# Dilated score products on 64 rows of the array, items in pairs of heads

## What is computed

```
q_nope, q_rope = q[..., :64], rope(q[..., 64:96])          # "mla": 96 features a head
s = (q_nope @ k_nope + q_rope @ k_rope) * 96 ** -0.5       # causal, blocks of 128 queries
o_mla = softmax(s) @ v_mla                                 # 64 features a head
qd, kd, vd = 8 heads of 64 features; qd, kd = rope(qd), rope(kd)
o_dil = mix over windows (128, 1), (512, 4), (2048, 16) of softmax(qd @ kd) @ vd
```

## Time and profile before

| | |
|---|---|
| median of 3 runs | 3322.12 us (3318.78 to 3323.09) |
| the profiled execution | 3324.39 us, of which the span of the profile is 3322.6 us |
| mean granted TensorE clock | 0.959 of full |
| PE, PEld busy | 3011.2 us (91%), 2524.6 us (76%) |
| DVE, ACT, POOL busy | 1620.6 us (49%), 1219.5 us (37%), 296.5 us (9%) |
| DMA | mean 73 GB/s |

### The profile page before, as it was taken

How to read it: one execution, slowest core, us unless ns; L and a number is a source line. 1 busy time by engine, 2 the same in 40 slices (tenths; PEclk the granted TensorE clock), 3 DMA queues, 4 the chain that set the end, 5 groups by cost and what they waited for, 6 DMA issues and landing times. The chain is left out here.

```text
span 3322.6 us, 40007 instructions
## 1 busy us (share of the span) xinstructions
PE 3011.2 (91%) x15598; PEld 2524.6 (76%) x15598; DVE 1620.6 (49%) x2744; ACT 1219.5 (37%) x2044; POOL 296.5 (9%) x274
## 2 busy tenths in 40 slices
PE   5798879989799999978899999899999778999997
PEld 3676879868578888855688888788888646888886
DVE  5744455442544443536564434654435275644336
ACT  4423544322333322335543323533223345432224
POOL 0000057620000000011000000000000020000000
PEclk9899989999899999989999999999999899999998
DMA  7111000012223333210123232132332200233321
GB/s 240 57 58 44 1 12 1 1 32 95 63 76 104 101 96 101 89 51 1 49 78 97 95 102 95 58 108 95 96 107 83 70 1 33 72 100 98 99 95 58
DMA packets 66860, 241.95 MB, mean 73 GB/s; under 512 B 7408, under 2 KB 9584, under 8 KB 66032
## 3 DMA queue, kind: packets, MB, share of 16 engines
q1 hardware_dynamic: 66672, 239.38, 22.3%
HBM read 236.21 MB, written 3.15 MB: 72 GB/s over the span
## 5 line engine op out<-in xcount | busy, mean ns | idle before, releaser
L220 PE MATMUL pair<-h_hi_at,w_hi_at 128*128 128x512 f32 (+1 forms) x2048 | 782.1, 382 | 45.4 <-DVE h_lo_at L410 30.6
L222 PE MATMUL pair<-h_hi_at,w_lo_at 128*128 128x512 f32 (+1 forms) x2048 | 760.5, 371 | 0.0
L221 PE MATMUL pair<-h_lo_at,w_hi_at 128*128 128x512 f32 (+1 forms) x2048 | 760.4, 371 | 0.0
L188 DVE TENSOR_TENSOR w_lo_at<-w_raw,w_hi_at 128x1024 fp32r<-128x1024 f32 x350 | 436.8, 1251 | 472.2 <-ACT w_hi_at L180 472.1
L180 ACT ACTIVATE w_hi_at<-w_raw 128x1024 fp32r<-128x1024 f32 x350 | 366.0, 1052 | 537.1 <-PE pair L222 521.3
L220 PEld LDWEIGHTS pair<-h_hi_at,w_hi_at 128*128 128x128 f32 x2048 | 389.8, 190 | 121.7 <-DVE h_lo_at L410 37.0
L221 PEld LDWEIGHTS pair<-h_lo_at,w_hi_at 128*128 128x128 f32 x2048 | 390.3, 191 | 67.1
L222 PEld LDWEIGHTS pair<-h_hi_at,w_lo_at 128*128 128x128 f32 x2048 | 389.9, 190 | 65.4
L2144 DVE TENSOR_TENSOR work_at<-pair,rstd_at 128x512 f32<-128x512 f32 (+1 forms) x184 | 122.1, 667 | 363.4 <-PE pair L222 363.3
L220 PE MATMUL pair<-a_hi_at,w_hi_at 128*128 128x512 f32 (+1 forms) x792 | 290.1, 366 | 0.0
L221 PE MATMUL pair<-a_lo_at,w_hi_at 128*128 128x512 f32 (+1 forms) x792 | 289.4, 365 | 0.0
(11 more groups left out here) (395 smaller groups left out, 4423.2 us busy)
## 6 DMA issues: line engine op xcount, KB each, us to landing
w_raw<-in_weights SPq DMA_DIRECT2D x433, 512.0 KB, 3.5
residual<-in_x SPq DMA_DIRECT2D x1, 2048.0 KB, 10.4
cos_sin_at<-rope_table SPq DMA_DIRECT2D x2, 1024.0 KB, 5.1
out<-residual SPq DMA_DIRECT2D x16, 128.0 KB, 1.7
rope_table<-table SPq DMA_DIRECT2D x1, 1024.0 KB, 11.1
ctx_in<-in_ctx SPq DMA_DIRECT2D x1, 1024.0 KB, 5.0
mask_at<-in_layer_masks SPq DMA_DIRECT2D x2, 512.0 KB, 4.3
levels<-in_levels SPq DMA_DIRECT2D x1, 896.0 KB, 4.5
```

The lines of the kernel that those rows point to most:

```text
L188: eng.tensor_tensor(self.w_lo[:, g % self.split].rearrange("p k n -> p (k n)"), self.w_raw[:, g % RAW], self.w_hi[:, g % self.split].rearr ...
L220: pe.matmul(out, sh, mh, start=start, stop=False)
L221: pe.matmul(out, sh, ml, start=False, stop=False)
L222: return pe.matmul(out, sl, mh, start=False, stop=stop)
```

## The change

The padded copy goes away: `qd` is rotated in place, as one addition of 128 rows a tile, and the instruction that clears `q_wide` is left out. The score product of a dilated item takes 64 rows of `qd` and the same 64 rows of `kd`: rows 0 to 63 for an even head, 64 to 127 for an odd one. The items of both kinds come in pairs of heads: two heads of block 0, the same two of block 1, and so on, so that widths run 128, 128, 256, 256, 384, 384, 512, 512. PE's order becomes one by pairs: `score(i)`, `score(i + 1)`, `turn(i - 2)`, `turn(i - 1)`, `weigh(i - 4)`, `weigh(i - 3)`. The programs of DVE and ACT and all waits are unchanged.

```diff
-def rope(kit, items, clear, copy=None, room=None):
+def rope(kit, items, clear=None, copy=None, room=None):
...
-                act.activation(clear, kit.squares[:, 0, 0:1][:, :, None].to_broadcast(clear.shape), ACT.Copy,
-                               scale=0.0).then_inc(cleared, 1)
+                if clear is not None:
+                    act.activation(clear, kit.squares[:, 0, 0:1][:, :, None].to_broadcast(clear.shape), ACT.Copy,
+                                   scale=0.0).then_inc(cleared, 1)
...
-def attention(kit, items, sink, room=None):
+def attention(kit, items, sink, room=None, paired=False):
...
+                if paired:
+                    for i in range(0, n + 4, 2):
+                        for job, j in ((score, i), (turn, i - 2), (weigh, i - 4)):
+                            if 0 <= j < n:
+                                job(j)
+                                job(j + 1)
+                    return
                 lag = ahead - 1
                 for i in range(n + lag + 2):
...
-         + [(qd[:, t], [(rows, q_wide[rows, 2 * t + i]) for i, rows in enumerate(halves)], dil) for t in range(4)],
-         clear=q_wide[:, :, :], copy=(kh[HD:HD + 32, :, :],
+         + [(qd[:, t], qd[:, t], dil) for t in range(4)],
+         copy=(kh[HD:HD + 32, :, :],
...
-    kinds = ((qh[0:96], kh[0:96], 1, vm, o_lat, (HD + 32) ** -0.5), (q_wide, kd, 2, vd, o_dil, HD ** -0.5))
-    items = [dict(head=h, q=q[:, h, n * P:(n + 1) * P], pieces=[(k[:, h // per_tile, 0:(n + 1) * P], 0)],
...
-    attention(kit, items, sink=False, room=Room(kit, H_UNIT))
+    def item(kind, head, n, q, k, v, out, scale):
...
+    items = [item(0, h, n, qh[0:96, h], kh[0:96, h], vm, o_lat, (HD + 32) ** -0.5)
+             for t in range(4) for n in range(4) for h in (2 * t, 2 * t + 1)]
+    items += [item(1, 2 * t + i, n, qd[rows, t], kd[rows, t], vd, o_dil, HD ** -0.5)
+              for t in range(4) for n in range(4) for i, rows in enumerate(halves)]
+    attention(kit, items, sink=False, room=Room(kit, H_UNIT), paired=True)
```

More of the change, by code:

```diff
@@ L2713, in interior @@
     project_kv(kit, (lat_split[0][:, 2], lat_split[1][:, 2]), kh, vm)
-    q_wide = kit.delta
     halves = (slice(0, HD), slice(HD, P))
@@ L2719, in interior @@
          + [(kd[:, t], kd[:, t], dil) for t in range(4)]
-         + [(qd[:, t], [(rows, q_wide[rows, 2 * t + i]) for i, rows in enumerate(halves)], dil) for t in range(4)],
-         clear=q_wide[:, :, :], copy=(kh[HD:HD + 32, :, :],
+         + [(qd[:, t], qd[:, t], dil) for t in range(4)],
+         copy=(kh[HD:HD + 32, :, :],
                                       k_rope[HD:HD + 32, :][:, None, :].to_broadcast([32, 8, SEQ])), room=Room(kit, WORK_UNIT))
-    kinds = ((qh[0:96], kh[0:96], 1, vm, o_lat, (HD + 32) ** -0.5), (q_wide, kd, 2, vd, o_dil, HD ** -0.5))
-    items = [dict(head=h, q=q[:, h, n * P:(n + 1) * P], pieces=[(k[:, h // per_tile, 0:(n + 1) * P], 0)],
-                  width=(n + 1) * P, values=[v[:, b, h * HD:(h + 1) * HD] for b in range(n + 1)],
-                  mask=mask[:, kind, 512 - (n + 1) * P:512], out=out[:, n, h * HD:(h + 1) * HD], scale=scale)
-             for kind, (q, k, per_tile, v, out, scale) in enumerate(kinds) for h in range(8) for n in range(4)]
-    attention(kit, items, sink=False, room=Room(kit, H_UNIT))
+    def item(kind, head, n, q, k, v, out, scale):
+        w = (n + 1) * P
+        return dict(head=head, q=q[:, n * P:w], pieces=[(k[:, 0:w], 0)], width=w, scale=scale,
+                    values=[v[:, b, head * HD:(head + 1) * HD] for b in range(n + 1)], mask=mask[:, kind, 512 - w:512],
+                    out=out[:, n, head * HD:(head + 1) * HD])
+    items = [item(0, h, n, qh[0:96, h], kh[0:96, h], vm, o_lat, (HD + 32) ** -0.5)
[3 more added lines that the diff above has]
+    attention(kit, items, sink=False, room=Room(kit, H_UNIT), paired=True)
     at = layer * KD
```

## The result

The changed kernel takes 3475.43 us (median of 4 runs, 3470.45 to 3478.35), the kernel before 3322.61 us beside it. The ratio is 1.046, with a 95% interval of 1.0442 to 1.0478. It is 153 us slower where 54 were forecast: the direction was right, the size about a third of what came. The profiled execution has a span of 3471.8 us and a mean TensorE clock of 0.921 (before: 0.959).

What follows compares the result with a forecast made beforehand. PE was taken as the bound; the new order's round trip adds 29.9 us a layer, rope takes off 2.9, so 27.0 a layer, 54.0 in all: 3376.1 us, range 3355 to 3403.

Steps and rivals of the forecast that it cites:

- What bounds the kernel: Attention stage: PE's real work at full clock is the bound, busy 94.6 of 98.7 us.
- the pairing pays: Rival: attention stays bound by PE's work, rope's 2.9 and scores' 8.5 us come off per layer, 3299 us; chance 0.05.
- Rope: Rope stage, bound by DVE: single additions 1.89 us apart, last 0.69 us long; stage ends 2.9 us earlier.
- Score products: Dilated half: 64-row pairs save 8.5, 4.3 or 0 us of PE time a layer, hidden beside the round trip.
- the drain: Dilated half: changing PE's tiling mode drains the engine, 0 to 4.2 us a layer; taken as 0.
- Order of PE: Attention: each pair costs a full round trip, rounds 3.71, 4.40, 3.34, 4.45 us; stage 128.6 against 98.7 us.
- the named wait: Attention: turn(i - 1) waits for item i - 3's copy, behind exp(i) on ACT; over 1 us each.
- the loop: Attention: round trip from a pair's scores through DVE and ACT back to PE, 15.9 us per two heads against 11.8.
- The clock: Attention: PE's clock stays at 1.00, as in rope when busy 1.12 of 2 us; chance of a fall 0.08.
- The clock's price: Dilated half at clock 0.50: PE terms double, 7.5 us more per two heads, 60 us in all.
- The range: Total time: 3355 to 3403 us, widened from 3358 to 3400, leaving out a clock fall.
- the clock case: Rival: clock falls to 0.50 in the dilated half, 60 us more, total 3436 us; chance 0.08.

Runs made afterwards that it cites:

- e2: Changed kernel with PE's old order (score i, turn i-3, weigh i-5), 64-row products and paired items kept: 3331.93 us, ratio 1.0038.
- e3: Changed kernel with a deeper pair order: scores i, i+1, turns i-3, i-2, weighs i-5, i-4: 3319.37 us, ratio 0.9997.
- e8: Changed kernel with PE order score i, i+1, turn i-3, weigh i-5, turn i-2, weigh i-4: 3306.97 us, ratio 0.9956.
- e9: Changed kernel with padded queries and 128-row scores back, PE order score i, i+1, turn i-3, weigh i-5, turn i-2, weigh i-4: 3316.48 us.
- e6_same: Changed kernel with dilated pairs made of two heads on the same 64 rows, so their score products can't overlap: 3475.87 us, ratio 1.0462.
- e1_order: Changed kernel with padded queries and 128-row score products back, pair order kept: 3415.03 us, ratio 1.0283.
- e5_act: Changed kernel with ACT's copy of item i-3 moved ahead of the exponential of item i: 3368.4 us, ratio 1.0138.
- e4_fill: Changed kernel with one unused 128 x 384 PE product added between the two turns of every pair: 3384.7 us, ratio 1.0194.

## Why the prediction was wrong

- **What bounds the kernel**: right. PE's own work bounds the stage, and every order that kept PE from waiting long (e2, e3, e8, e9) came out within 0.5% of before. e8_mix, at 3307 us, comes near the 3299 of the rival *the pairing pays*, by an order that the change didn't have.
- **Rope**: right, and exact: 36.3 to 33.4 us in both layers, with additions 1.89 us apart and a last one of 0.69 us.
- **Score products**: three values stood, and the drain was taken at 0. The overlap is full, and the switch costs about 0.24 us a time. That the saving is hidden in the changed order was right: serial and side-by-side scores give the same time (e6_same). The switch is hidden only in part: 0.14 us a round, 2.2 us a layer, within the range of 0 to 4.2. The row that was taken as the reason for 0, a 128-wide score ahead of a transpose of 128 rows, has no change of rows in it and couldn't show one.
- **Order of PE**: right. Rounds at full clock are 3.76, 4.51, 3.34 and 4.47 us against 3.71, 4.40, 3.34 and 4.45 (the second and third read in e1_order, 1587.80 to 1592.31 to 1595.65), and 0.14 us more each with 64-row pairs. e5_act took the named wait away and 107 us with it, e4_fill shows the loop at nearly full clock: 3385 against the forecast 3376.
- **The clock**: this step failed. The forecast kept 1.00 and gave the fall a chance of 0.08. The reason given was the rope stage, busy 1.12 of 2 us at clock 1.00, against 57 to 70% busy in the new rounds. A busy share of one mix of products was carried to another. Rope's products are 512 columns over 128 rows; the rounds are transposes, weighs of 64 columns and scores over 96 rows (mla) or 64, with a standstill of up to 1.4 us in the mla half. Windows of 2 us of the changed kernel show the first fall, right behind the longest standstill (1527.7 to 1529.1):

```profile
1528.00:1530.00 2.00, 0.90 (x5) 0.80 (x6) 0.96 (x6) 1.45 (x5) 0.00 (x0) 0.91 0.04 12
1530.00:1532.00 2.00, 2.00 (x11) 2.00 (x11) 0.00 (x0) 0.28 (x1) 0.00 (x0) 0.50 0.00 0
```

The next falls, at 1550, 1571 and 1591 us, stand beside the same wait, each in a round of width 256. The wait at the first of them:

```profile
1549.84 0.30 PE L1223 MATMUL pair<-squares,probs_at 128*128 128x128 f32 x1 [1.38 <-ACT probs_t_at L1318]
```

- **The clock's price** was right where I gave one: 23.4 us per two heads, 24.2 measured, and 60 us for the dilated halves, where the changed kernel takes 28 and 30 us a layer more than e4_fill (102.7 against 74.7 and 72.9). Its reach was not. The rival had it in the dilated half alone; the mla half fell too, and takes 73.6 and 75.5 us where e4_fill takes 60.6 and 61.1. Loop and clock together are 176 to 178 us a stage, of which e4_fill's 134 to 135 are the loop (with the change of rows and what is left of the clock's falls) and 41 to 44 the clock. Of the 99 us by which the forecast missed, the clock is so some 85, and the loop, forecast at 128.6 us a stage, some 12.
- **The range** ended at 3403 because the clock case was left out of it. Its upper end should have covered that rival: here the loop that made PE wait was also what put its clock at risk (e4_fill). Its low end doesn't follow from its sum either: 3376 less 10 is 3366, and 3358 was written.

What stays open: what of a product's shape keeps the clock up, whether it is the rows of the scores or the changes between row counts that come with them, and why the dilated half with 128 rows (e1_order) held a mean of 0.95 when the mla half with 96 rows in the same order didn't. That 64-row work in itself doesn't bring the clock down is shown: in e2_rows and e3_lag, where PE stands for 0.7 us at the most, it stayed at 1.00 through the dilated halves.

## What to carry to other kernels

When an order of work is changed on one engine, write down for each wait what stands ahead of the awaited instruction on the other engine. A lag shorter by one item closed a round trip here, and one item more gave it all back (e3_lag: 156 us). Where PE gets new standstills, price the stage at both clock levels, and don't infer the clock from a busy share read at other shapes. Side-by-side products over 64 rows overlap in full, but the changes of rows and a wait for a store took nearly all of that back (e8_mix against e9_mix_pad: 0.17 us of 11 per two heads), and switched to one at a time they lose (e2_rows: 6.5 us a dilated half).

## What the runs showed of the hardware

- Two fp32 products over the two 64-row halves take the time of one: 1.06 us for four records (e3_lag) as for two (e2_rows), at width 512.
- Going from 128-row to 64-row products and back costs about 0.24 us (e2_rows against before). Behind a wait 0.14 us of it still show (e4_fill against e1_order).
- The clock fell to 0.50 behind standstills of 1.38 us, with PE busy 0.90 of 2 us around the first (changed kernel, mla half).
- PE was busy 95.3 of 99.6 us at a mean clock of 0.54 (e6_same, 64-row scores). Pairs with 128-row scores in the same order of PE ran at 0.95 (e1_order), and dense 64-row work that started at 1.00 stayed there (e2_rows).
- Useless work can be a gain: 32 products of 128 x 384 more in each attention stage took 91 us off the changed kernel, by the clock (mean of the stage 0.95 and 0.98 instead of 0.60 and 0.58).
